# Feed-forward gate and up projections: the high weights against high and low stream columns in one 512-wide matmul

## What is computed

```python
D_MODEL = 1024; SEQ = 256; D_FF = 2816
# first block, for l in range(2), after the mixer
up = depthwise_conv(h @ ffn_w_up[l], ffn_conv_w[l], ffn_conv_b[l])      # three taps
f = (jax.nn.silu(up[..., :D_FF]) * up[..., D_FF:]) @ ffn_w_down[l]
h = layer_norm(DEEPNORM_ALPHA * h + f, ln_ffn_g[l], ln_ffn_b[l])
...
def swiglu(h, wi, wo):
    gate, up = jnp.split(h @ wi, 2, axis=-1)
    return (jax.nn.silu(gate) * up) @ wo
# second block, for i in range(2)
x = x + 0.5 * swiglu(rms_norm_2(x, ffn1_norm[i]), ffn1_wi[i], ffn1_wo[i])
...
x = x + 0.5 * swiglu(rms_norm_2(x, ffn2_norm[i]), ffn2_wi[i], ffn2_wo[i])
```

## Time and profile before

| | |
|---|---|
| median of 3 runs | 2011.35 us (2008.17 to 2011.93) |
| profiled execution | 2011.94 us, its span 2010.2 us |
| PE busy | 1887.2 us (94%), 12484 matmuls |
| DVE busy | 1262.0 us (63%) |
| ACT busy | 903.0 us (45%) |
| POOL busy | 103.0 us (5%) |
| weights and data moved | 310.82 MB, 155 GB/s |
| mean granted TensorE clock | 0.955 of full speed |

### The profile page before, as it was taken

One profiled execution on the slowest core, in us unless ns is written; L12 is line 12 of the kernel. 1 busy time (PEld: TensorE's weight loads), 2 busy tenths in 40 slices (PEclk: granted clock), 3 DMA queues, 4 the chain that ended last, 5 costly groups with the idle time before them and its releaser, 6 DMA issues.

```text
span 2010.2 us, 31242 instructions
## 1 busy us (share of the span) xinstructions
PE 1887.2 (94%) x12484; PEld 1701.4 (85%) x12484; DVE 1262.0 (63%) x1571; ACT 903.0 (45%) x1086; POOL 103.0 (5%) x79
## 2 busy tenths in 40 slices
PE   7989999988999999999988999999999987799999
PEld 6965899985699989998986788999999875689998
DVE  5786876788787777555546646555655555546555
ACT  4444544444454444334443355333533465545332
POOL 0300200030020000000041000000000000000000
PEclk9997999998999999999986999999999997899999
DMA  9540455542155545554621435555555531235553
GB/s 296 190 132 22 163 194 188 188 140 105 63 189 185 183 154 170 188 188 146 191 85 63 168 127 168 187 188 188 168 188 184 171 106 63 71 119 168 188 188 126
DMA packets 226932, 310.82 MB, mean 155 GB/s; under 512 B 6630, under 2 KB 199430, under 8 KB 226214
## 3 DMA queue, kind: packets, MB, share of 16 engines
q1 hardware_dynamic: 224038, 298.07, 44.4%
q0 software_dynamic: 2528, 10.14, 1.6%
q10 hardware_dynamic: 288, 1.54, 0.2%
HBM read 306.57 MB, written 3.15 MB: 154 GB/s over the span
## 4 chain that ended last, share of the span: by engine, by line
PE 85%; DVE 7%; ACT 4%; issue 2%; POOL 1%; DMA 1%; DVEq 0%; ACTq 0%
PE bank L675 43%; PE bank L905 17%; PE bank L798 8%; PE bank L698 3%; PE bank L684 3%; PE bank L947 1%; PE bank L971 1%; DVE work L1922 1%; ACT w_hi L1392 1%; DVE w_lo L1925 1%; PE bank L731 1%; DVE work L1925 1%; PE bank L1214 1%; PE bank L958 1%; DVE x L1922 1%
## 5 line engine op out<-in xcount | busy, mean ns | idle before, releaser
L1925 DVE TENSOR_TENSOR w_lo<-raw,w_hi 128x2048 fp32r<-128x2048 f32 x280 | 641.9, 2300 | 387.2 <-ACT w_hi L1392 386.7
L1392 ACT ACTIVATE w_hi<-raw 128x2048 fp32r<-128x2048 f32 x280 | 533.0, 1904 | 699.9 <-PE bank L675 445.8
L675 PE MATMUL bank<-xt_hi,w_hi 128*128 128x256 f32 x2560 | 727.7, 284 | 0.9 <-DVE w_lo L1925 0.9
L675 PE MATMUL bank<-xt_lo,w_hi 128*128 128x256 f32 x2560 | 725.4, 283 | 0.0
L675 PE MATMUL bank<-xt_hi,w_lo 128*128 128x256 f32 x2560 | 725.2, 283 | 0.0
L675 PEld LDWEIGHTS bank<-xt_hi,w_hi 128*128 128x128 f32 x2560 | 491.6, 192 | 7.6 <-issue 3.2
L675 PEld LDWEIGHTS bank<-xt_lo,w_hi 128*128 128x128 f32 x2560 | 491.5, 192 | 2.4 <-issue 0.2
L675 PEld LDWEIGHTS bank<-xt_hi,w_lo 128*128 128x128 f32 x2560 | 491.5, 192 | 0.0
L905 PE MATMUL bank<-w_hi,act_hi 128*128 128x512 f32 x528 | 206.5, 391 | 0.0
L905 PE MATMUL bank<-w_lo,act_hi 128*128 128x512 f32 x528 | 206.1, 390 | 0.0
L905 PE MATMUL bank<-w_hi,act_lo 128*128 128x512 f32 x528 | 205.4, 389 | 0.0
(11 more groups left out here) (302 smaller groups left out, 2117.7 us busy)
## 6 DMA issues: line engine op xcount, KB each, us to landing
raw<-in_ffn_wi SPq DMA_DIRECT2D x88, 1024.0 KB, 5.1
raw<-in_ffn_w_up SPq DMA_DIRECT2D x44, 1024.0 KB, 5.1
raw<-in_ffn_wo SPq DMA_DIRECT2D x44, 1024.0 KB, 4.8
raw<-in_ffn_w_down SPq DMA_DIRECT2D x22, 1024.0 KB, 5.4
raw<-in_w_in SPq DMA_DIRECT2D x14, 1024.0 KB, 5.4
raw<-in_ssd_in_proj SPq DMA_DIRECT2D x14, 1024.0 KB, 5.4
raw<-in_mem_wkv SPq DMA_DIRECT2D x9, 1024.0 KB, 7.5
raw<-in_w_out SPq DMA_DIRECT2D x8, 1024.0 KB, 5.2
```

The costliest lines, as they stand in the source:

```text
L675: ins = first(mm(dst, w[s][:, k, c0:c0 + m], xt[v][:, k, :], start=k == 0 and p == 0, stop=k == KT - 1 and p == 2))
L1392: return act.activation(dst, src, ACT.Copy)
L1925: return dve.tensor_tensor(out=out, in0=in0, in1=in1, op=op)
```

## The change

PE makes gate and up units in another form. The two stream buffers become one, `xt`, in which the 256 high and the 256 low columns of a slice stand side by side. For each tile and slice the high weights then meet all 512 columns in one matmul, and the low weights meet the 256 high columns in a second one, so that a unit has 32 matmuls (16 of 512 columns and 16 of 256) in place of 48 of 256. The 512-wide result fills a bank: columns 0 to 255 hold high times high, and the low weights' product is added there; columns 256 to 511 hold the high weights times the low stream. Somebody has to add the two halves.

- A unit takes two banks, one for each tile: gate banks 0 and 1, up banks 2 and 3, with no second set. PE starts a gate (up) unit when DVE has emptied the one before (`pair_drained`), and the first one of a feed-forward waits for two banks of the turned stream, where it waited for one.
- ACT copies the low half of both banks to `f_low` (`low_half`), one instruction of 128x512 for each unit. DVE adds the high half to it (`whole`), one instruction of 128x512.
- In the second kind the sum goes to `f_gate` or `f_up`; the multiplication by `rb` and the product with silu then read these. That is two more DVE instructions and two more ACT instructions a chunk.
- In the first kind the sum goes to `f_sum`, and centre and side taps read it there. Centre taps now wait for DVE's sum. In the loop the split of gate c+1 moves behind the sum of gate c on DVE, and the split of up c+1 moves behind silu on ACT.
- The row of scale factors goes to bank 4. It is spread behind gate 0, but behind up 0 in `ffn1.0`, the first feed-forward of the second block. ACT copies it between two splits.

```diff
-        xt_hi = sb("xt_hi", [P, KT, T], F32R)
-        xt_lo = sb("xt_lo", [P, KT, T], F32R)
+        xt_both = sb("xt", [P, KT, 2, T], F32R)
+        xt_hi = xt_both[:, :, 0, :]
+        xt_lo = xt_both[:, :, 1, :]
...
+            def wide_tiles(b, w, first, done):
+
+                def tile(k, j):
+                    dst, part = bank[b + j], slice(P * j, P * j + P)
+                    first(mm(dst[:, :], w[0][:, k, part], xt_both[:, k, :, :], start=k == 0, stop=False,
+                             skip_group_check=True))
+                    ins = mm(dst[:, 0:T], w[1][:, k, part], xt_hi[:, k, :], start=False, stop=k == KT - 1,
+                             skip_group_check=True)
...
+                def spread_rows():
                     pe.wait_ge(row_ready, seen.next(row_ready))
-                    claim(1, f"{tag}.rb")
+                    claim(4, f"{tag}.rb")
...
+                for i in range(2):
+                    for b in (2 * i, 2 * i + 1):
+                        pe.wait_ge(bank_drained[b], names.fills[b])
+                    up_pair(i, i, None)
+                    if scaled and i == (1 if tag == "ffn1.0" else 0):
+                        spread_rows()
...
-                        for b, kk in ((c % 2, k), (2 + c % 2, k + 1)):
-                            pe.wait_ge(bank_drained[b], base[b] + i)
-                            up_pair(kk, b, i)
-                        down(k + 2, c - 1, i)
+                        for i in range(2):
+                            pe.wait_ge(pair_drained[i], turn * 2 + chunk_count(tag, c - 1))
+                            up_pair(k + i, i, turn)
+                        down(k + 2, c - 1, turn)
...
+            def low_half(tag, what, c, turn):
+
+                i = "gu".index(what)
+                act.wait_ge(pair_full[i], chunk_count(tag, c) if turn is None else turn * 2 + chunk_count(tag, c))
+                copy(f_low[:, 2 * i:2 * i + 2, :], psum[:, 2 * i:2 * i + 2, T:2 * T]).then_inc(low_ready, 1)
...
+            def whole(tag, what, c, turn, dst):
+
+                i = "gu".index(what)
+                dve.wait_ge(low_ready, seen.next(low_ready))
+                dve.wait_ge(pair_full[i], chunk_count(tag, c) if turn is None else turn * 2 + chunk_count(tag, c))
+                tt_(dst, psum[:, 2 * i:2 * i + 2, 0:T], f_low[:, 2 * i:2 * i + 2, :],
+                    ALU.add).then_inc(pair_drained[i], 1)
...
-                    tt_(f_gate[:, c % 2, :, :], two(bank[b][:, :]), spread(rb[:, :], 2),
-                        ALU.mult).then_inc(bank_drained[b], 1)
+                    whole(tag, "g", c, turn, f_gate[:, c % 2, :, :])
+                    tt_(f_gate[:, c % 2, :, :], f_gate[:, c % 2, :, :], spread(rb[:, :], 2),
+                        ALU.mult).then_inc(gate_ready, 1)
...
-                    taps(c, f"{tag}.g{c}", f_gate, 0, turn)
-                    taps(c, f"{tag}.u{c}", f_up, 22, turn)
+                    total(c, "g", turn)
+                    if turn is not None:
+                        split_in_loop(tag, 3 * c + 2, turn)
+                    taps(c, "g", f_gate, 0, turn).then_inc(taps_ready, 1)
+                    total(c, "u", turn)
+                    step(taps(c, "u", f_up, 22, turn))
```

More of the change, by code:

```diff
@@ L207, in weight_units, with chunk_count @@
     return place
+FFN_ORDER = ("conv0", "conv1", "ffn1.0", "ffn2.0", "ffn1.1", "ffn2.1")
+def chunk_count(tag, c):
+    return NCHUNK * FFN_ORDER.index(tag) + c + 1
 class Count:
@@ L299, in sem @@
             return ctx.enter_context(nc.semaphore(name))
-        bank = [ctx.enter_context(nc.psum_tensor(f"bank{b}", [P, HALF], F32)) for b in range(8)]
+        psum = ctx.enter_context(nc.psum_tensor("bank", [P, 8, HALF], F32))
+        bank = [psum[:, b, :] for b in range(8)]
         raw = sb("raw", [P, RING, UNIT])
@@ L518, in mixed_block_kernel @@
         row_ready = sem("row_ready")
+        pair_full = [sem(f"pair_full_{w}") for w in "gu"]
+        pair_drained = [sem(f"pair_drained_{w}") for w in "gu"]
+        low_ready = sem("low_ready")
+        gate_ready = sem("gate_ready")
+        taps_ready = sem("taps_ready")
         qsum_ready = sem("qsum_ready")
@@ L701, in both_tiles @@
                 return ins
+            def wide_tiles(b, w, first, done):
[5 more added lines that the diff above has]
+                             skip_group_check=True)
+                    if k == KT - 1 and j == 1:
+                        ins.then_inc(done, 1)
+                if stream_due:
+                    for k in range(KT):
+                        stream_tile(k)
+                        for j in range(2):
+                            tile(k, j)
+                else:
+                    for j in range(2):
+                        for k in range(KT):
+                            tile(k, j)
             def pair_fm(unit, b, name):
@@ L1552, in ffn @@
                         split_in_loop(tag, 3 * c + 2, i)
-                        chunk(c, f"{tag}.g{c}", i)
+                        chunk(c, i)
                         split_in_loop(tag, 3 * c + 3, i)
+                    seen.leave(TURNS)
                 after_ffn(tag)
@@ L1566, in center @@
                         at = bass.ds(44 + t, 1) if turn is None else bass.ds(turn * 4 + 44 + t, 1)
[L1567 removed]
+                        ins = act.activation(dst[:, c % 2, j, :], f_sum[:, 2 * i + j, :], ACT.Identity,
                                              scale=par[:, cw, at], bias=par[:, cb, at])
@@ L2215, in convffn, with total, taps @@
                 wa, wb = prow[f"ffn_conv_w{l}a"][0], prow[f"ffn_conv_w{l}b"][0]
-                steps_per_chunk = 4
-                def taps(c, name, dst, tile0, turn):
+                steps_per_chunk = 5
+                def total(c, what, turn):
+                    i = "gu".index(what)
+                    whole(tag, what, c, turn, f_sum[:, 2 * i:2 * i + 2, :])
+                def taps(c, what, dst, tile0, turn):
                     dve.wait_ge(center_ready, seen.next(center_ready))
-                    b, n = names.of[name]
+                    i = "gu".index(what)
                     for g, side in ((wa, 0), (wb, 1)):
@@ L2226, in taps @@
                             part = dst[:, c % 2, j, 1:T] if side == 0 else dst[:, c % 2, j, 0:T - 1]
-                            src = bank[b][:, T * j:T * j + T - 1] if side == 0 else bank[b][:, T * j + 1:T * j + T]
+                            src = f_sum[:, 2 * i + j, 0:T - 1] if side == 0 else f_sum[:, 2 * i + j, 1:T]
                             ins = stt(part, src, w, part, ALU.mult, ALU.add)
```

80 lines of the change are left out of this document (36 added, 44 removed).

## The result

| | before | after |
|---|---|---|
| median | 2011.07 us of 4 runs (2008.17 to 2011.93) | 2025.48 us of 4 runs (2016.89 to 2028.14) |
| profiled execution, its span | 2011.94, 2010.2 us | 2016.89, 2015.1 us |
| mean granted clock of the profiled execution | 0.955 | 0.954 |
| matmuls | 12484 | 10372 |
| DVE, ACT busy | 1262.0, 903.0 us | 1341.9, 976.8 us |

The change makes the kernel slower: the ratio is 1.0068, with a 95% interval of 1.0049 to 1.0088, 10 to 18 us. The forecast was 2008.2, with 2000 to 2016 around it. The profiled execution of after is the fastest of its four; the other three spans are 2022.0 to 2026.3 us at mean clocks of 0.949 to 0.952.

A forecast was written before the change was run, and what follows sets the result against it. PE was taken to bound the loops, with slack elsewhere mattering only at feed-forward starts and ends. A 25.1 us gain less losses of 3.8, 13.2, 3.2 and 1.2 left 3.7: 2008.2 us, range 2000 to 2016.

The forecast's parts named there:

- The gain, 25.1 us: Gate and up units: a wide and a narrow matmul take 0.3478 us for 0.3597, saving 25.1 us over 132 units.
- The argument on the fixed part of a matmul: All matmuls: each has 13 to 15 ns independent of width, against the skill's about 2.5 ns, an estimated 5.3 us gain.
- fourth rival: Gate and up units: a wide matmul costs what two narrow ones do, 0.2398 us; 25.1 gain gone, 2033 us; chance 0.06.
- Loops: nothing: Inside the chunk loops: the extra DVE and ACT work costs zero, as PE's 16.6 us covers DVE's 14.8.
- End of conv0 and conv1, 1.9 each: At down 10, PE waits 2.1 us for chunk 10's own result where it waited 0.2; loss 3.8 us for both.
- Start of conv0 and conv1, 6.6 each: PE waits 0.6 us at gate 1, 4.5 at down 0, 1.5 at up 2; loss 13.2 us for both.
- second rival: Half clock after new waits at down 0 of conv0 and conv1 and at ffn1.0; 2009 to 2013 us; chance 0.17.
- Start of ffn1.0, 3.2: Gate 1 needs gate 0's sum, which stands behind two DVE splits, and starts at 773.5, not 770.3; loss 3.2 us.
- The other three starts, 1.2: Gate 0 of ffn2.0, ffn1.1 and ffn2.1 waits 0.4 us longer for bank 1; loss 1.2 us for three.
- The sum: Whole kernel: gain 25.1 less losses 3.8, 13.2, 3.2 and 1.2 leaves 3.7 us, giving 2008.2.
- rivals on POOL: Start of conv0 and conv1: taps and POOL hinder each other less than assumed; 1998.8 to 2004.6 us; chance 0.22.
- on DVE as the bound: Conv loops: DVE's chain exceeds 16.6 us; at 17.6, 20 chunks lose 1.0 each, 2028 us; chance 0.08.

The follow-up runs named there:

- form_alone_8: Kernel before with only PE's new matmuls, a tile's eight wide ahead of its eight narrow except in each feed-forward's first unit; 1983.08 us against 2008.34, ratio 0.9871.
- form_alone: Kernel before with only PE's new wide and narrow matmuls in turn, banks, DVE, ACT and waits as before; 2002.47 us against 2009.06, ratio 0.9956.
- runs_of_8: Changed kernel with each tile's eight wide matmuls ahead of its eight narrow ones, except in a feed-forward's first unit; 2012.08 us, ratio to before 1.0025.
- narrow_again: Changed kernel with its banks, sums, copies and waits, but three 256-column matmuls for a tile and slice again; 2039.58 us, ratio 1.0132 to before.
- bank1_wait: Kernel before, with gate 0 of second-kind feed-forwards also waiting for bank 1 to be empty; 2012.77 us against 2008.34, ratio 1.0022.
- late_bank: runs_of_8 with conv0 and conv1 as before; second-kind gate 0 starts with its first tile, waiting for bank 1 at slice 3; 1993.92 us, ratio 0.9931.
- late_bank_order: late_bank, with ffn1.0's gate 0 low half copied between ACT's two splits and summed between DVE's two; 1991.54 us, ratio 0.9911.
- all_fixed: late_bank_order with conv0 and conv1 in the wide form too, their sums written back into the bank; 2002.24 us, ratio 0.9965.

## Why the prediction was wrong, point by point

**The gain, 25.1 us: the step that failed.** I took the price of a wide matmul from a row of down units, where only wide ones follow each other, and that of a narrow one from gate units of narrow ones, and added them up to 0.3478 us a pair. The order that the diff writes puts one behind the other in turn, and no row of before had that. It costs 0.353. The period fell by 0.19 us and not 0.38, for 66 chunks 12.5 us and not 25.1. The argument on the fixed part of a matmul was right all the same: form_alone_8 gives 25 us. By the fixed part of about 2.5 ns that the Trainium skill, "TensorE: Matmul & The Clock Gate", section "Back-to-back issue gap", gives for an isolated warm matmul, the gain would be an estimated 5 us. No run here agrees: form_alone has 9 and form_alone_8 25. My fourth rival was a wide matmul as dear as two narrow ones, 0.3597 a pair. The measured pair lies halfway between that and my sum: the gain came off by a half, not by the whole.

**Loops: nothing.** Right. PE is busy throughout, DVE 13.24 of 16.79 us, and form_alone and the changed kernel have the same period.

**End of conv0 and conv1, 1.9 each.** Right in kind, too small in size. Down 10 starts 8.4 us after down 9, whose matmuls take 5.5, so it waits 2.9 where it waited 0.2 before (5.64 and 5.47). The loss is 2.7. From up 10's start to `act_lo` are 13.8 us, where I had 13.1; the handovers from ACT to DVE take 0.1 to 0.2 us each, and I had left out most of them.

**Start of conv0 and conv1, 6.6 each.** In runs_of_8, where gate 0 ran at full clock as I had assumed, gate 1, up 1, down 0 and up 2 are late by 0.6, 2.4, 1.6 and 1.9 us, 6.5 in all. The sum was right to 0.1 us by luck, its parts were not: I had 4.5 at down 0 and nothing at up 1, which waits for the sum of up 0 behind the hindered taps. Nor is the 1.6 a wait: behind its new wait up 1 itself runs at a mean clock of 0.76 there. In narrow_again's conv0 it runs at full clock, and down 0 waits 1.4 instead, so half clock costs next to nothing at this place, as the second rival had it. In the changed kernel's trace gate 0 of both runs at half clock (7.53 and 7.55 us). That costs 1.9 us each. It also puts DVE's split behind POOL's first instruction (2.29 us where the earlier trace rows have 4.01), and the delays are 1.2 at up 1, 1.5 at down 0 and 1.8 at up 2. Up 2 starts 6.5 us later than in form_alone, so the total is the same again.

**Start of ffn1.0, 3.2.** Gate 1 starts 18.7 us after gate 0 and started 15.9 after it before, 2.9 later; I had 3.2 less 0.38. Behind it gate 1 runs at half clock, 1.6 us more. This is the second rival, and here it came as told. All eight traces with this start (18.7 us) have half clock on gate 1. But so have form_alone and bank1_wait, where gate 1 starts 15.9 us after gate 0 as in the kernel before, so the 1.6 is not shown to be the price of the new wait.

**The other three starts, 1.2.** The wait is 0.4 us as forecast, the cost is not: 4.4 us in bank1_wait. I looked for half clock behind new waits of 4 us and not behind one that was there and grew by a quarter.

**The sum.** Gain 12.6 less than forecast, ends 1.6 more, bank 1 3.2 more, ffn1.0 1.6 more, conv starts 0.2 less: 18.8 us from a sum that had -3.7, so +15.1, beside +14.4 measured (10 to 18). So two thirds of the miss are the gain, and most of the rest is half clock. The rivals on POOL and on DVE as the bound did not come about: taps and POOL took turns, and DVE's chain fitted.

**What stays open.** Why alternation costs PE 5 to 6 ns a pair. And whether half clock on gate 0 of conv0 and conv1, where no wait of this change stands ahead, is chance. PE's stops ahead of it are the same in every kernel (3.69 and 1.74 to 1.92 us). Of 28 such gates in 14 traces 11 were hit, both in the changed kernel and none in the kernel before, but also one in form_alone_8, late_bank and late_bank_order each, whose conv0 and conv1 have no new wait. In nine of the 11 the 16 matmuls between the two stops had run at half clock to their end; in the 17 that were not hit the clock had risen within them (mean 0.52 to 0.58), as it had in the two of all_fixed. That speaks for chance, by where the stretches of half clock lie, and does not settle it; the medians of four to twenty runs even it out only in part.

## What to carry to other kernels

Price a matmul from rows with the same neighbours, not only the same shape: where wide and narrow ones are to be mixed, write them in groups of at least two. When a change lengthens a stop of PE ahead of a long stretch of work, even by 0.4 us, count the clock too, and let PE start with what is there. An accumulator that two engines have to sum costs most where there is no next unit to hide it, at the starts and ends, so it belongs where the chain behind it is short.

## What the runs showed of the hardware that I had not expected

- Alternating matmuls of 512 and 256 columns, each with its own weights, cost 0.353 us a pair at full clock (starts 236 and 117 ns apart). In groups of two or eight equal ones they cost 0.348 (1.81 + 0.95 us and 1.84 + 0.95 us for the two runs of eight).
- Ahead of gate 0 of ffn2.0, ffn1.1 and ffn2.1, 2.10 to 2.50 us without a new matmul brought half clock (1.2 GHz, 1.4 to 1.6 us lost) in 13 of 24 cases, 1.70 to 2.06 us in none of 18. This holds for these places alone: ahead of gate 0 of conv0 and conv1, where PE had stopped for 3.69 us shortly before, 1.74 to 1.92 us brought it in 11 of 28.
- DVE's addition with one operand in the bank and one in SBUF takes 0.68 to 0.69 us beside GpSimd's instructions of 128x1024, as if these weren't there. Of four taps with two SBUF operands the two that met one of them took 2.61 and 2.50 us in place of 0.47. A cast with one SBUF operand was held up as well, 2.52 us in place of 0.43.
